# A two-block transformer kernel: smaller pieces of a projection behind every indexer row, the key projection second, and two small jobs in a later stage

## The reference

```python
h = rmsnorm(x, norm_mix[layer])
proj = h @ w_in[layer]
qa, ka, va, qb, kb, vb, qi, ki, wi, ga, gb = jnp.split(proj, IN_OFFSETS, axis=-1)
qa = rope(qa.reshape(B, T, A_HEADS, HEAD_DIM), pos)
ka = rope(ka.reshape(B, T, A_HEADS, HEAD_DIM), pos)
y_a = dilated_mixture(qa, ka, va)
qi = rope(qi.reshape(B, T, IDX_HEADS, IDX_DIM), pos)
ki = rope(ki[:, :, None], pos)[:, :, 0]
y_b = indexed_sparse_attention(qb, kb, vb, qi, ki, wi)
# inside indexed_sparse_attention, for a block of 128 queries:
dots = jnp.einsum('bqhd,bsd->bqhs', qi_blk, ki)
score = jnp.einsum('bqh,bqhs->bqs', wi_blk, jax.nn.relu(dots)) * IDX_SCALE
_, sel = lax.top_k(score, topk)
```

## Time and profile before

| | before |
|---|---|
| median of 3 runs | 3267.68 us (3265.21 to 3273.69) |
| the profiled execution, its own time | 3261.15 us |
| its span | 3259.4 us |
| PE busy | 2987.7 us (92%) |
| DVE busy | 1751.2 us (54%) |
| ACT busy | 1227.4 us (38%) |
| POOL busy | 1246.9 us (38%) |
| mean granted TensorE clock | 0.963 |

### The profile page before, as it was taken

How to read it: one execution, slowest core, us unless ns; L and a number is a source line. 1 busy time by engine, 2 the same in 40 slices (tenths; PEclk the granted TensorE clock), 3 DMA queues, 4 the chain that set the end, 5 groups by cost and what they waited for, 6 DMA issues and landing times. The chain is left out here.

```text
span 3259.4 us, 36545 instructions
## 1 busy us (share of the span) xinstructions
PE 2987.7 (92%) x13886; PEld 2299.6 (71%) x13886; DVE 1751.2 (54%) x2625; ACT 1227.4 (38%) x1810; POOL 1246.9 (38%) x698
## 2 busy tenths in 40 slices
PE   7778888889989999999998899997889999999998
PEld 5555556566678788888886566665677788878886
DVE  4467777766223544445495554566553554455544
ACT  3345554454433333333133344455554322231110
POOL 4331334212133597776246300032102697732221
PEclk8889999899999999999999999998999999999999
DMA  6411102111143123323231311010002233343222
GB/s 178 113 46 27 39 23 62 40 39 52 40 163 102 52 77 92 82 77 116 81 111 42 113 39 32 17 43 7 20 4 84 59 116 103 117 154 103 90 78 65
DMA packets 278270, 236.11 MB, mean 72 GB/s; under 512 B 22709, under 2 KB 250933, under 8 KB 277557
## 3 DMA queue, kind: packets, MB, share of 16 engines
q1 hardware_dynamic: 278136, 234.42, 24.3%
HBM read 170.91 MB, written 53.51 MB: 69 GB/s over the span
## 5 line engine op out<-in xcount | busy, mean ns | idle before, releaser
L921 PE MATMUL big<-g_hi,w_hi 128*128 128x512 f32 (+1 forms) x2112 | 701.1, 414 | 71.4 <-ACT gst_b L1424 21.1
L2361 POOL TENSOR_TENSOR w_lo<-w_raw,w_hi 128x1024 fp32r<-128x1024 f32 x147 | 356.3, 2424 | 925.8 <-ACT w_hi L1315 924.2
L921 PE MATMUL big<-g_lo,w_hi 128*128 128x512 f32 (+1 forms) x2112 | 667.0, 398 | 0.0
L921 PE MATMUL big<-g_hi,w_lo 128*128 128x512 f32 (+1 forms) x2112 | 664.9, 396 | 0.0
L921 PEld LDWEIGHTS big<-g_hi,w_hi 128*128 128x128 f32 (+1 forms) x2112 | 380.8, 193 | 225.5 <-issue 150.8
L921 PEld LDWEIGHTS big<-g_lo,w_hi 128*128 128x128 f32 (+1 forms) x2112 | 405.0, 192 | 90.3 <-issue 0.6
L921 PEld LDWEIGHTS big<-g_hi,w_lo 128*128 128x128 f32 (+1 forms) x2112 | 403.8, 191 | 90.4 <-issue 0.4
L1315 ACT ACTIVATE w_hi<-w_raw 128x1024 fp32r<-128x1024 f32 x147 | 154.7, 1053 | 406.4 <-PE big L921 378.4
L1343 ACT ACTIVATE a_hi<-a_raw 128x512 fp32r<-128x512 f32 x114 | 72.1, 632 | 334.2 <-POOL a_raw L2368 329.4
L1179 PE MATMUL big<-b_hi,a_hi 128*128 128x512 f32 x456 | 178.6, 392 | 8.3 <-DVE b_lo L2162 6.1
L1179 PE MATMUL big<-b_hi,a_lo 128*128 128x512 f32 x456 | 177.9, 390 | 0.0
(11 more groups left out here) (334 smaller groups left out, 5572.3 us busy)
## 6 DMA issues: line engine op xcount, KB each, us to landing
a_spill<-c SPq DMA_DIRECT2D x54, 512.0 KB, 3.3
g_lo<-a_spill SPq DMA_DIRECT2D x54, 512.0 KB, 4.7
w_raw<-in_w_in SPq DMA_DIRECT2D x51, 512.0 KB, 4.5
w_raw<-in_w_down SPq DMA_DIRECT2D x40, 512.0 KB, 3.7
w_raw<-in_w_up SPq DMA_DIRECT2D x27, 512.0 KB, 5.9
u_raw<-in_w_up SPq DMA_DIRECT2D x27, 512.0 KB, 6.0
rot<-rope_in SPq DMA_DIRECT2D x68, 128.0 KB, 2.3
g_spill<-gst_b SPq DMA_DIRECT2D x16, 512.0 KB, 3.0
```

The lines of the kernel that those rows point to most:

```text
L921: ins = pe.matmul(out[0:m, HALF * h:HALF * h + HALF], w[slot][:, col:col + m], x[:, HALF * h:HALF * h + HALF], start=(n == 0 and q == 0), ...
L2361: pool.tensor_tensor(w_lo[s][:, :], w_raw[s][:, :], w_hi[s][:, :].bitcast(F32), ALU.subtract).then_inc(*s_wlo.mark(w))
```

## The change

The list `S` is rearranged, and the weaving is made finer.

- `kiwi` is projected second, straight after `qi0`, and `qi1` third. `wi_t`, `iparts 0` and `kparts` come before `qi2`. The load of `kiwi` gets a third copy that fills the last 56 columns of its buffer.
- `qi3` is no longer projected by itself but woven into the first `idx` stage; then come `qa0`, `ka0` and `va0`. `qa1` moves to the first head pair of the dilated stage, which so has three woven products in place of two.
- Behind every row of `idx` there are now 4 matmuls (two of a block's three pairs), 12 times, instead of 6 matmuls 8 times.
- `lam` is split: `lamp` (the DVE products) stands behind unit 3 of the dilated stage, `lam` behind unit 5.
- The four `b_spill` copies are issued one at a time, each at the fifth unit (i = 4) of a head pair of the dilated stage. `masks`, `norm_gains` and `head_gains` move to the stages `qi2`, `qa0` and `ka0`.

```diff
-    mixed("kiwi", w_in, [(0, KI, HD), (HD, WI, 8)])
+    mixed("kiwi", w_in, [(0, KI, HD), (HD, WI, 8), (HD + 8, KI, HD - 8)])
...
     add("rope", "qi0")
     add("ss", "mix")
     add("tables", "b1")
+    add("kiwi")
     add("rope", "qi1")
-    add("kiwi")
+    add("wi_t")
     add("iparts", 0)
+    add("kparts")
     add("rope", "qi2")
-    add("wi_t")
-    add("kparts")
-    add("rope", "qi3")
     add("iparts", 1)
-    for c, name in enumerate(("va0", "qa0", "ka0", "qa1")):
+    for c, name in enumerate(("qi3", "qa0", "ka0", "va0")):
         stage = "lin" if name == "va0" else "rope"
         add("begin", stage, name)
         add("idx", c)
         add(stage, name)
         if c < 2:
             add("iparts", c + 2)
-        if c == 1:
-            add("lam")
...
-            filler[8 * c] = ([("rope", f"qa{c + 1}")] if c else []) + [("rope", f"ka{c + 1}"), ("lin", f"va{c + 1}")]
+            filler[8 * c] = [("rope", f"qa{c + 1}"), ("rope", f"ka{c + 1}"), ("lin", f"va{c + 1}")]
...
+    late[3], late[5] = [("lamp",)], [("lam",)]
...
-        def weave(points=1):
+        def weave(points=1, pairs=0):
+
+            n = pairs or 3 * points
...
-                        if i % 3 != 1:
-                            weave()
+                        weave(pairs=2)
...
-            elif stage == "wi_t":
-                for h in range(4):
+            elif stage == "sc" and x[0][0] == "a" and x[0][2] == 4:
+                for h in (x[0][1],):
                     sp.wait_ge(*s_bsp[h].at(h))
                     sp.dma_start(b_spill[h].rearrange("(p m) -> p m", p=P),
```

More of the change, by code:

```diff
@@ L913, in passes @@
[L913 to L923 removed]
+        def weave(points=1, pairs=0):
+            n = pairs or 3 * points
+            if not job or job["done"] == 3 * len(job["terms"]):
+                return
+            w, total = W[job["name"]], 3 * len(job["terms"])
+            if job["done"] == 0:
+                pe.wait_ge(s_wlo.sem, w + 1)
+                take(job["key"], job["by"])
+                job["bank"] = pair[job["key"]]
+            ins = passes(big[pair[job["key"]]], job["m"], w % 2, job["terms"], job["done"], min(job["done"] + n, total))
+            job["done"] = min(job["done"] + n, total)
+            if job["done"] == total:
+                ins.then_inc(*s_big.mark(*job["key"]))
+                s_big.known[("w", w)] = s_big.count
+                finished(job["bank"])
+                job["bank"] = None
@@ new lines, in passes @@
+        def passes(out, m, slot, terms, first=0, last=None):
+            total = 3 * len(terms)
+            for p in range(first, total if last is None else last):
+                col, hi, lo, ready = terms[p // 3]
+                if ready is not None and p % 3 == 0:
+                    pe.wait_ge(*ready)
+                w, x = ((w_hi, hi), (w_hi, lo), (w_lo, hi))[p % 3]
+                for h in range(2):
+                    ins = pe.matmul(out[0:m, HALF * h:HALF * h + HALF], w[slot][:, col:col + m],
+                                    x[:, HALF * h:HALF * h + HALF], start=p == 0, stop=p == total - 1)
@@ L2625, in _ @@
                 swap((x[0],), zb, P, s_arel.at(x[0]))
[L2626 removed]
+                if x[0] == "qi2":
                     masks()
[L2628 removed]
+                elif x[0] == "qa0":
                     norm_gains()
[L2630 removed]
+                elif x[0] == "ka0":
                     head_gains()
```

30 lines of the change are left out of this document (2 added, 28 removed).

## The result

| | before | changed |
|---|---|---|
| median | 3266.44 us of 4 runs (3263.43 to 3273.69) | 3229.22 us of 4 runs (3224.09 to 3235.16) |
| the profiled execution, its own time | 3261.15 us | 3235.16 us |
| ratio, with its 95% interval | | 0.9883 (0.9857 to 0.9910) |

The change made the kernel 37 us faster; 33 were forecast (3234.4, range 3224 to 3246). A second measurement of the same kernel, in a later group of runs, gave 0.9889 (0.9874 to 0.9903). In all fourteen profiles of this document, what comes after the first scores with `qb0` (some 520 to 560 us from the start) is untouched by the edits, and yet it takes between 2697.9 and 2709.6 us.

The account below looks back on a forecast made before the run. PE was taken as the bound, with time won only where it stands or runs at the lower clock; terms summed to -33.3 us, from the median 3267.68 to 3234.4 us, range 3224 to 3246.

Parts of the forecast that it names:

- The kiwi load: Ahead of the first product: three narrow copies of `kiwi`, loaded among the first, cost +0.9 us; bounds 0 and +3.5.
- The way to the second row: Ahead of the first index stage: the reordered products bring the second index row to 91.5 us from 118.21, -26.7 us.
- masks and gains: 0: Moving these small loads into the index stages costs 0, as SP idles over 20 us in each.
- The finer weave: Index stages: twelve times four matmuls instead of eight times six wins 9.8 us, 3.3 given back, so -6.5; bounds 0 and -9.8.
- row model: Index rows: the larger of ACT's and PE's time per row, summed over six rows, 10.6 us against 11.8 before.
- heads 10.6 to 11.2 us apart: Index stages: sign expected in the changed profile, with stands of PE within a head under 0.5 us.
- some of this reaches PE (1.3 in all): Index stages: GpSimd's rotation of `qi3` and DVE's slow `idx_acc` beside GpSimd give back 1.3 us of the weave's gain.
- Steps between the stages: Between index stages: first +0.1, second -6.8 without `lam`, third -1.1 without `qi_parts` and `rope_in` wait; -7.8 us in all.
- `va0` last: Before the first dilated scores: PE waits for ACT's read and GpSimd's product of `va0` before transposing, +2.5 us.
- `qa1` and `lam` in the dilated stage: First dilated head pair: `qa1` adds +3.8 us, partly filling PE's stands, bounds +1.5 and +10.9; `lam` adds +0.5.
- The bias copies: Dilated stage: the moved copies cost 0, since exchanged halves behind them are needed only some 17 us later.
- the rival of 4 x 10 us: Dilated stage: each bias copy holds the next halves or weight piece 10.0 us, 40 in all: 3274.4 us; chance 0.03.

Follow-up runs that it names:

- uneven weave: Changed kernel with 12 woven matmuls behind an index stage's first row, 2 or 4 behind others, none behind the second head's first: 3232.52 us, ratio 0.9885.
- coarse weave: Changed kernel with the old grain, 6 woven matmuls behind four of the six index rows instead of 4 behind all six: 3230.98 us, ratio 0.9896.
- order back: Changed kernel with the old order of the products; finer weave, late bias copies and late `lam` kept: 3243.43 us, ratio 0.9923.
- qi split inside: Changed kernel with `iparts` between an index stage's two heads, one-copy `kiwi` load, earlier `w_lo` of `qi1`, `va0` transposes behind the first scores: 3227.21 us, ratio 0.9869.
- masks and gains early: Changed kernel with the small loads of masks, gains and vectors issued at `qi0`, `qi1` and `qi2` again: 3234.82 us, ratio 0.9899.
- search prepared late: Changed kernel with `va0` transposes behind the first two score parts and DVE's search preparation behind the first minimum of the dilated stage: 3225.42 us, ratio 0.9865.
- `lam` back: Changed kernel with `lamp` and `lam` back behind the second index stage, masks and gains loaded early again: 3241.04 us, ratio 0.9917.

## Why the prediction was right

**The kiwi load, +0.9.** The first product starts 0.76 us later in the first profile and 0.89 in the second (35.17 and 35.30 against 34.41); with one copy in place of three it starts at 34.49. So the cause is shown and the size is right, but not the working: the issue was put at 2.6 us and took 5.36, 3.6 more than the one copy, which is the upper bound that was given for packets alone. And what stands ahead did not cost DVE "directly". The first copy of x to memory was issued 3.7 us later (23.07 against 19.41), yet DVE, which waits for it, went on at 26.93 and not at 26.17:

```profile
26.93 1.29 DVE L1879 COPY xs<-obank 128x512 f32<-128x512 f32 x2 [4.88 <-issue]
```

Two errors of about 2.8 us cancel in this term, which is luck; why the copy landed so much sooner after its issue no run shows.

**The way to the second row, -26.7, with the kiwi term -25.8.** Measured 118.21 - 92.21 = 26.0, and 24.9 in the second profile. That is 70% of the effect. Moving the bias copies alone is worth 9 us (taken back) or 13 (done alone), and the order of the products 12 net of what it costs later. The step behind "masks and gains: 0" was incomplete: their new places cost nothing, but leaving the old ones is worth 3.4 us, since in the new order these loads would stand between the exchanged halves of `qi1` and the `qi_parts` copies that PE waits for. The number of the change is unaffected, as the forecast stepped through a queue without them; who kept the new order and left them in place would lose it.

**The finer weave, -6.5.** Mis-sized: 3.1 as a mean over seven profiles, 6.1 in the first one alone. The row model's 1.2 us a head came in the second heads of three stages (1.1) and not in all eight heads. Of the 9.8 that it gave, not 3.3 but about 6.7 are given back. The sign "heads 10.6 to 11.2 us apart" failed accordingly: the first heads last 15.3 us in the second and third stage. The step that failed is "some of this reaches PE (1.3 in all)" for DVE beside GpSimd: DVE's three slow `idx_acc` take 5.7 us longer than alone, in the first head of each stage, and the uneven weave showed that PE's work does not set the length there; that DVE beside GpSimd does is read from the rows.

**Steps between the stages, +0.1, -6.8, -1.1.** Measured 0.0, -6.9, -1.3 (6.13, 6.15 and 3.98 against 6.12, 13.04 and 5.25). The reason given for the third, that the first row goes without `rope_in`, is what the rows above show. What brings it about is the finer weave and not the order of the products, since the step is as short with the old order (3.99) and long with the coarse weave (5.94).

**`va0` last, +2.5.** Measured from the last index row to the first woven matmul: 8.81 against 5.93, +2.9.

**`qa1` and `lam` in the dilated stage, +4.3.** Mis-sized. From the last index row to the transposes of the earlier trace rows at 295.38 it took 67.5 us before and 71.7 after (72.4 in the second profile); less the 2.9 of `va0` that is +1.2 to +2.0. The added blocks nearly all went into the stands of 3.56 and 3.65 us and into PE's half-clock time: the pair's clock rose from 0.89 to 0.99. `lam` itself waited 0.4 us. The forecast stopped at the transposes and so missed what follows: the second head pair lasts 77.1 to 77.9 us in the three profiles with the old order of products (before, bias copies moved, order back) and 73.5 to 75.1 in ten of the eleven with the new one, the changed kernel's first profile (77.6) being the exception. From the last index row to the third head pair it took 140.8 to 141.5 us with the old order and, less the 2.9 of `va0`, 140.3 to 142.0 in five profiles that have the changed kernel's order and woven products there, and 144.6 in the changed kernel's first. So in most executions `qa1` and `lam` cost next to nothing there.

**The bias copies, 0,** and the rival of 4 x 10 us: refuted by distances of 15.2 us and more, landings of 4.6 to 8.3 us, and -13 us when they move alone.

**The sum** up to the transposes was to be -33.3; the first profile has -36.1, the second 265.76 - 295.38 = -29.6. Over several profiles the gain of the weave was put too high by 3 and the cost of `qa1` too high by 2 to 3, and the two cancel. So the total was right partly by luck. What the forecast didn't see is what follows after it: at the first scores with `qb0` the two profiles of the changed kernel are only 27.9 and 25.9 us ahead (530.66 and 532.65 against 558.59), and yet the medians differ by 36 to 37 us. The profiled execution of the kernel before was itself 5 to 9 us under that kernel's medians. One fortunate part of it can be named: its fourth head pair lasted 111.3 us, where the same code took 116.7 with only the bias copies moved, and 116.9 and 116.3 in the changed kernel. Against a pair of the long kind the first profile would be 33 us ahead. How often each kind comes in whole runs, and so how the rest of the 37 us is made up, stays open, as there is one profile of the kernel before only.

## What to carry to other kernels

A large copy is best moved away from a point where a small copy is waited for next, and it pays to ask again after every reordering which copy that is: here it was a weight piece before, and two copies of 256 KB after. Before more work is dealt out to fill a stand, look at the engine two steps up the chain, since a stand that another engine causes only changes its place. And where an effect of some 3 us is to be judged, take several profiles, as one profile of one kernel had 79 and the next 84 us for the same 44 rows.

## What the hardware showed that was not expected

**Tiny instructions of DVE that wait for a whole instruction of GpSimd.** The fourth head pair, to the first scores with `qb0`, lasts 110.3 to 111.3 us in five profiles (before, coarse weave, qi split inside, masks and gains early, search prepared late) and 116.2 to 117.1 us in the other nine, and nothing in between. It goes with `flip` and `edge`, two instructions of the search on 128x2 elements: in the nine long ones an `edge` some 39 to 40 us into the pair takes 2.2 us, in the five short ones, where it comes at 38 to 39 us, it takes 0.16. Timelines of DVE and GpSimd with masks and gains early:

```profile
450.66 2.39 POOL L2419 TENSOR_TENSOR rot<-rot,sin_r 64x1024 f32<-64x1024 f32 x1 [25.93 <-DMA rot<-rope_in]
...
452.44 0.64 DVE L2021 TENSOR_SCALAR flip<-above 128x2 int32<-128x2 f32 x1
...
453.11 0.16 DVE L2026 SCALAR_TENSOR_TENSOR edge<-flip,edge 128x2 int32<-128x2 int32 x1
453.13 2.40 POOL L2423 TENSOR_TENSOR kb_b<-rot,rot 64x1024 f32<-64x1024 f32 x1
```

The same instructions in the changed kernel's second profile, and PE behind them:

```profile
453.31 2.35 POOL L2423 TENSOR_TENSOR kb_b<-rot,rot 64x1024 f32<-64x1024 f32 x1
...
453.49 2.26 DVE L2021 TENSOR_SCALAR flip<-above 128x2 int32<-128x2 f32 x1
...
455.63 2.35 POOL L2359 TENSOR_TENSOR w_lo<-w_raw,w_hi 128x1024 fp32r<-128x1024 f32 x1
455.78 2.22 DVE L2026 SCALAR_TENSOR_TENSOR edge<-flip,edge 128x2 int32<-128x2 int32 x1
...
460.53 0.49 PE L1086 MATMUL big<-ka,qa 64*128 64x128 f32 x4 [4.04 <-DVE mn_part L2079]
```

In the first `flip` ends at 453.08, as a product of GpSimd ends at 453.05, and `edge` slips in before the next has a hold. In the second `flip` comes 0.2 us after that product has begun and takes 2.26 us, until it has ended at 455.66; `edge` behind it meets the next one and takes 2.22. PE stands 4.04 us for what is queued behind them, its next matmuls run at half clock, and by the end of the pair the long kind is 5.8 us behind the short one (means of nine and of five). Between these two profiles a shift of 0.9 us between DVE and a transfer that GpSimd waits for makes the difference. The Trainium skill, SBUF — State Buffer, Who interferes with whom, says that VectorE and GpSimd share a pair of ports as an exclusive lock, and that a VectorE instruction with two SBUF inputs contends with a GpSimd instruction that reads SBUF. `edge` has two such inputs, and the trace agrees, down to an operation of two columns (2.22 us in place of 0.16). `flip` has one; for such an instruction the section has contention only in the modes that use both ports, which a `tensor_scalar` can enter. The trace shows that `flip` was held for 2.26 us, and no run here shows its mode. From these rows the rival on contention would be priced by the number of meetings, each up to one GpSimd instruction (2.4 us here), and not by a share of 2 us a stage.

**The granted clock falls in some executions of the same program and not in others.** The mean clock of the whole execution and its time go together: of 11 runs of the kernel before in one group, ten had 3262.7 to 3273.4 us at 0.962 to 0.966 and one 3256.1 us at 0.968. In the stretch from 35 to 60 us, where PE runs the same products in these three, it was 0.87 with `lam` back, 0.92 in the changed kernel and 1.00 with the coarse weave. What decides it no run here shows.
